# Three probability buffers instead of four in the first attention of a two-block transformer kernel

## Chip, core and metric

One Trainium2 chip, one of its cores. The metric is the device time of one launch in microseconds (us), the median of several runs. All arithmetic is float32, the large matrix products as three products of split operands. The engines that matter here are TensorE (PE), ScalarE (ACT), VectorE (DVE) and GpSimd (POOL). Each works through its own list of instructions in order and waits on semaphores that the others raise.

## What is computed

The reference is a chain of two transformer models of two layers each on 256 latent and 256 context tokens of width 1024. The change touches only the attention of the very first layer (`even_mixer`): eight heads of global grouped-query attention and eight heads of neighbourhood attention with a bias table, each over 512 keys for the latent tokens and over 256 keys for the context tokens. Cut to what matters:

```python
def gqa_scores(q, k):
    return jnp.einsum('bqkgd,btkd->bkgqt', q, k).astype(jnp.float32)

def gqa_out(p, v):
    return jnp.einsum('bkgqt,btkd->bqkgd', p.astype(v.dtype), v)

# global_gqa, heads 0..7 (latent queries see context and latent keys)
p = jax.nn.softmax(gqa_scores(q, k_all), axis=-1)
y = gqa_out(p, v_all)
# context queries see context keys alone
p = jax.nn.softmax(gqa_scores(qc, k_ctx), axis=-1)
y_ctx = gqa_out(p, v_ctx)
# neighbourhood_attention, heads 8..15: the same with a bias and a window on the latent keys
s_nb = jnp.einsum('brwhd,brwyxhd->bhrwyx', qblk, kn) + bias[None]
p = jax.nn.softmax(jnp.concatenate([s_nb, s_ctx], -1), axis=-1)
```

## The kernel before

The whole kernel is one long program for each engine: projections, attention, output rows, feed-forward layers, four times over. The change lies in the first attention stage, which in the profile runs from 134.6 to 226.5 us.

**Units.** The stage is cut into 24 units (`units_of("ev")`), three for each pair of heads: latent tokens 0 to 127 (t=0), latent tokens 128 to 255 (t=1), and all 256 context tokens (t=2, "context unit"). In units 0 to 11 the heads are global; from unit 12 on they are neighbourhood heads, whose t=0 and t=1 units are of the kind "rpb" (with the bias table). The words used below are: a *plain* unit is t=0 or t=1 of the first half, a *bias* unit is t=0 or t=1 of the second half.

**The steps of unit i.**

- scores(i), PE, L670: four matmuls of 256 columns (the trace counts eight records) into one of two pairs of PSUM banks. It waits for exp(i-2), which frees the banks.
- max(i), DVE: one `tensor_reduce` (L2272); for a bias unit a shorter `tensor_reduce` (L2264) and two fused add-and-reduce operations (L2269).
- exp(i), ACT, L1525: two activations of 512 columns, or four of 256 for a context unit, each with a row sum, from PSUM into a place for probabilities `A.P[slot]` in SBUF.
- normalise(i): DVE computes the reciprocals (L2284) and scales the first head (L2289: one operation of 512, or two of 256); POOL scales the second head (L2931).
- transposes(i), PE, L679: eight 128x128 transposes of the probabilities into PSUM banks 4 and 5.
- turned(i), ACT, L1515: two copies of the transposed probabilities to SBUF.
- values(i), PE, L692: the products with the values.
- After the third unit of a head pair: mixed_high on ACT (L1539) and mixed_low on DVE (L2296) split the result into two parts.

**What sets the order.** No scheduler: each engine's list is written by a loop over i, and the distance between the steps is `A.lag`, one less than the number of places in `A.P`. With four places, lag is 3. The loops in a pass i are, for PE: scores(i), `fill(i)`, transposes(i-lag), values(i-lag-1). For ACT: mixed_high(i-lag-2), turned(i-lag), exp(i), `fill(i)`. For DVE: normalise(i-lag+1), max(i), mixed_low(i-lag-2), `fill(i)`. For POOL: normalise(i-lag+1), `fill(i)`. These are the lines on DVE:

```python
            for i in range(A.n + A.lag + 2):
                if 0 <= i - A.lag + 1 < A.n:
                    normalise(i - A.lag + 1)
                ahead(i)
                if i < A.n:
                    softmax(i)
```

where `normalise(i)` begins with a wait for exp(i), and `softmax(i)` on DVE is max(i).

**What is filled in between.** PE computes a last projection (48 matmuls of 256 columns, L515 to L517) in pass 1 and again in pass 2, and twelve matmuls of the output rows (`first_rows_out`, the `drain`) in pass n+lag-1, before the last transposes. ACT rounds a half of an output weight block (L1467, `weights_half`) after exp(15), exp(17), exp(19) and exp(21), and DVE subtracts it (L1982) one pass later. POOL prepares the bias tables (L2968, `masks`): four in pass 5, two in pass 16, two in pass 19.

The four places are two in the arena (`P4a`), the scratch tile `tmp`, and a further piece of the arena at offset 18432. The second attention stage of the kernel ("od") has its own four places.

Of the kernel before, what the change touches and what calls it, by code (L numbers as in the profile page):

```python
# [144 lines left out]
def build_program(nc, T):  # L145
    with ExitStack() as ctx:
        _build(nc, T, ctx)


def _build(nc, T, ctx):  # L150
    def sb(name, shape, dt=F):
        return ctx.enter_context(nc.sbuf_tensor(name, shape, dt))
# [10 lines left out]
    tmp = sb("tmp", [128, 2, 512])  # L163
# [36 lines left out]
    def AR(off, *shape):  # L200
        n = int(np.prod(shape))
        v = arena[:, off:off + n]
        if len(shape) == 2:
            return v.rearrange("p (a b) -> p a b", a=shape[0])
        if len(shape) == 3:
            return v.rearrange("p (a b c) -> p a b c", a=shape[0], b=shape[1])
        if len(shape) == 4:
            return v.rearrange("p (a b c d) -> p a b c d", a=shape[0], b=shape[1], c=shape[2])
        return v
# [223 lines left out]
    class Att2:  # L433
# [38 lines left out]

    P4a = AR(0, 2, 2, 512)
    ATT = {
        "ev": Att("ev", "ev", [P4a[:, 0, :, :], P4a[:, 1, :, :], tmp[:, :, :], AR(18432, 2, 512)], [AR(2048, 2, 512), AR(6656, 2, 512)]),
        "od": Att("od", "od", [AR(6656, 2, 512), AR(7680, 2, 512), AR(4608, 2, 512), AR(10240, 2, 512)],
                  [AR(13312, 2, 512), AR(0, 2, 512)]),
    }
# [2816 lines left out]
```

## Time and profile before

| | us |
|---|---|
| median of 3 runs | 1568.55 |
| lowest and highest | 1568.24, 1570.21 |
| the profiled execution, its own time | 1568.17 |
| its span (first to last instruction) | 1566.7 |
| PE busy | 1545.5 |
| DVE busy | 1068.5 |
| ACT busy | 884.1 |
| POOL busy | 335.3 |

The profile is of one execution. Its span lies 1.5 us under that execution's own time, and that time lies 0.4 us under the median. A row of the timeline shows the start, the duration, the engine, the line of the kernel, the operation, the tiles (written <- read), how many instructions are merged in the row, and in brackets how long the engine was idle just before and what ended that. The ends of matmuls are modelled, so the pace of PE is read from start to start.

### The profile page before, as it was taken

What the parts mean: (1) busy time and instruction counts of PE and PEld (TensorE: products, weight loads), DVE (VectorE), ACT (ScalarE), POOL (GpSimd) and SP (SyncE); (2) the same over time, 40 slices, a digit from 0 to 9 for tenths busy, and PEclk for the clock granted to TensorE, in tenths of its full rate; (3) what the DMA queues carried; (4) which work ended last, traced back from release to release, by engine and by line L of the source; (5) the groups of instructions that cost most, each with busy time, mean ns of one, the idle gap of its engine ahead of it and who ended that gap; (6) DMA issues with size and microseconds to landing.
All of it is one profiled execution on the core that took longest, in us unless ns stands there. A gap on an engine that the chain in (4) does not pass through costs nothing.

```text
span 1566.7 us, 25547 instructions
## 1 busy us (share of the span) xinstructions
PE 1545.5 (99%) x9942; PEld 1321.7 (84%) x9942; DVE 1068.5 (68%) x1989; ACT 884.1 (56%) x1741; POOL 335.3 (21%) x338
## 2 busy tenths in 40 slices
PE   7999999999999999999999999999999999999998
PEld 4788778988887888887999988988888898888887
DVE  4743766666444435788887778777888668779875
ACT  2423874666652423568455555766666557667663
POOL 0201430465540000012011102142221014412210
PEclk9999999999999999999999999999999999999999
DMA  9767123345667233021456562434555534435552
GB/s 377 292 239 247 16 88 134 117 183 211 227 224 274 81 108 137 26 82 68 169 183 227 188 232 102 145 108 163 187 189 189 205 138 143 154 135 189 188 202 81
DMA packets 46951, 260.35 MB, mean 166 GB/s; under 512 B 11888, under 2 KB 13296, under 8 KB 18160
## 3 DMA queue, kind: packets, MB, share of 16 engines
q1 hardware_dynamic: 43808, 252.59, 44.3%
q0 software_dynamic: 1296, 4.72, 0.8%
q8 instruction: 79, 1.29, 0.4%
q10 hardware_dynamic: 1728, 1.43, 0.3%
q14 instruction: 40, 0.33, 0.1%
HBM read 257.64 MB, written 1.07 MB: 165 GB/s over the span
## 4 chain that ended last, share of the span: by engine, by line
PE 93%; DVE 3%; DMA 1%; ACT 1%; issue 1%; POOL 0%; DVEq 0%; ACTq 0%; POOLq 0%
PE ps L515 22%; PE ps L517 22%; PE ps L516 22%; PE ps L775 8%; PE ps L776 5%; PE ps L670 2%; PE ps L692 2%; PE ps L679 2%; PE ps L531 2%; PE ps L1187 1%; PE ps L777 1%; DMA raw<-in_ada 1%; PE ps L578 1%; PE ps L1198 1%; PE ps L1214 1%
## 5 line engine op out<-in xcount | busy, mean ns | idle before, releaser
L1976 DVE TENSOR_TENSOR wl<-raw,wh 128x1024 fp32r<-128x1024 f32 (+2 forms) x304 | 357.6, 1217 | 248.1 <-ACT wh L1460 246.0
L1460 ACT CAST wh<-raw 128x1024 fp32r<-128x1024 f32 (+2 forms) x314 | 309.4, 1035 | 332.1 <-PE ps L517 299.3
L515 PE MATMUL ps<-xx,wh 128*128 128x256 f32 (+1 forms) x1006 | 328.1, 326 | 0.0
L517 PE MATMUL ps<-xx,wl 128*128 128x256 f32 (+1 forms) x1006 | 325.5, 324 | 0.0
L516 PE MATMUL ps<-xx,wh 128*128 128x256 f32 (+1 forms) x1006 | 325.4, 323 | 0.0
L515 PE MATMUL ps<-wh,xx 128*128 128x512 f32 (+2 forms) x782 | 286.5, 366 | 1.8 <-issue 0.8
L517 PE MATMUL ps<-wh,xx 128*128 128x512 f32 (+2 forms) x782 | 281.5, 360 | 0.0
L516 PE MATMUL ps<-wl,xx 128*128 128x512 f32 (+2 forms) x782 | 281.4, 360 | 0.0
L2346 DVE SCALAR_TENSOR_TENSOR arena<-ps,pv,arena 128x254 f32<-128x254 f32 (+2 forms) x352 | 192.8, 548 | 28.7 <-ACT arena L1660 19.3
L515 PEld LDWEIGHTS ps<-xx,wh 128*128 128x128 f32 x1006 | 191.2, 190 | 20.0 <-issue 3.6
L517 PEld LDWEIGHTS ps<-xx,wl 128*128 128x128 f32 x1006 | 191.2, 190 | 15.2
L516 PEld LDWEIGHTS ps<-xx,wh 128*128 128x128 f32 x1006 | 191.3, 190 | 14.7
L2955 POOL TENSOR_TENSOR arena<-arena 128x256 f32<-128x256 f32 (+1 forms) x88 | 97.8, 1111 | 435.1 <-ACT arena L1637 435.0
L775 PE MATMUL ps<-xx,wh 128*128 128x512 f32 x504 | 180.8, 398 | 0.0
L515 PEld LDWEIGHTS ps<-wh,xx 128*128 128x128 f32 x782 | 147.6, 189 | 31.6 <-issue 10.0
L517 PEld LDWEIGHTS ps<-wh,xx 128*128 128x128 f32 x782 | 147.5, 189 | 21.5
L516 PEld LDWEIGHTS ps<-wl,xx 128*128 128x128 f32 x782 | 147.8, 189 | 20.4
L776 PE MATMUL ps<-xx,wl 128*128 128x256 f32 x576 | 150.0, 281 | 0.0
L2901 POOL TENSOR_TENSOR st<-st,cs 128x1 f32<-128x1 f32 (+2 forms) x44 | 35.6, 809 | 432.5 <-DVE st L2159 222.0
L1660 ACT ACTIVATE arena<-ps,pv 128x256 f32<-128x256 f32 (+1 forms) x176 | 98.8, 611 | 47.8 <-DVE ps L2336 42.7
L776 PEld LDWEIGHTS ps<-xx,wl 128*128 128x128 f32 x576 | 108.7, 189 | 6.8
L775 PEld LDWEIGHTS ps<-xx,wh 128*128 128x128 f32 x504 | 94.8, 188 | 19.7
(255 smaller groups left out, 2246.7 us busy)
## 6 DMA issues: line engine op xcount, KB each, us to landing
raw<-in_ada SPq DMA_DIRECT2D x46, 1024.0 KB, 5.2
raw<-in_up SPq DMA_DIRECT2D x44, 1024.0 KB, 4.8
raw<-in_fin SPq DMA_DIRECT2D x44, 1024.0 KB, 4.8
raw<-in_down SPq DMA_DIRECT2D x22, 1024.0 KB, 4.8
raw<-in_fout SPq DMA_DIRECT2D x22, 1024.0 KB, 4.8
raw<-in_win SPq DMA_DIRECT2D x12, 1024.0 KB, 5.0
raw<-in_ev_w_in SPq DMA_DIRECT2D x9, 1024.0 KB, 8.4
raw<-in_wout SPq DMA_DIRECT2D x8, 1024.0 KB, 4.8
```

Of the source, the lines that this page charges most:

```text
L515: e.matmul(out, A[0], B[0], start=first, stop=False)
L516: e.matmul(out, A[0], B[1], start=False, stop=False)
L517: return e.matmul(out, A[1], B[0], start=False, stop=last)
L531: m = e.matmul(ps[b][32 * g:32 * g + 32, 0:256], silp[:, k, 14 - 2 * i:46 - 2 * i], wv[:, k, :], start=(i == 0 and k < 4), stop=(last and ...
L775: e.matmul(both, hv[:, k, fs], xx[:, :, k, 0:256], start=k == 0, stop=False)
L776: m = e.matmul(both[:, 1, :], lv[:, k, fs], xh[:, k, 0:256], start=False, stop=False)
L1460: e.copy(hi_of(j)[:, a:b], raw_of(j)[:, a:b]).then_inc(*S.hi.up((j, half)))
L1660: e.activation(temp(up, f)[:, part, 0:n], ps[2 * (f % 3) + part][:, 0:n], ACT.Identity, bias=w[3], scale=w[1 if up[0] == "u" else 2]).then ...
L1976: e.tensor_tensor(lo_of(j)[:, a:b], raw_of(j)[:, a:b], hi_of(j)[:, a:b].bitcast(F), ALU.subtract).then_inc(*S.lo.up((j, half)))
L2346: e.scalar_tensor_tensor(acc[:, :, lo:hi], src[:, :, lo + shift:hi + shift], conv(row, f + NT * part), acc[:, :, lo:hi], ALU.mult, ALU.add ...
L2901: e.tensor_tensor(out, in_, minus_half[:, 0:n], ALU.pow).then_inc(*S.gps.up(key))
L2955: e.tensor_tensor((ACTF if ngrp == 2 else ACTF1)[:, f, 0:n], t[:, 1, 0:n], t[:, 0, 0:n], ALU.mult).then_inc(*S.prod.up((up, f)))
```

## The change

The tile `tmp` is taken out of the list of places for probabilities of the first attention.

```diff
     ATT = {
-        "ev": Att("ev", "ev", [P4a[:, 0, :, :], P4a[:, 1, :, :], tmp[:, :, :], AR(18432, 2, 512)], [AR(2048, 2, 512), AR(6656, 2, 512)]),
+        "ev": Att("ev", "ev", [P4a[:, 0, :, :], P4a[:, 1, :, :], AR(18432, 2, 512)], [AR(2048, 2, 512), AR(6656, 2, 512)]),
```

As `lag` is `len(P) - 1`, it becomes 2, and all loops of the stage are written with the shorter distance: PE has scores(i), transposes(i-2), values(i-3) in a pass; ACT has mixed_high(i-4), turned(i-2), exp(i); DVE has normalise(i-1), max(i), mixed_low(i-4); POOL has normalise(i-1). The number of operations, their shapes and their operands are the same but for the place they write. No transfer is moved on the DMA queue of SP.

DVE, in the first half of the stage. `128x4` marks a context unit (L2272 is its max, L2284 and L2289 its normalise), `128x2` another unit. Before:

```order
L2272 TENSOR_REDUCE st<-ps 128x4
L2284 RECIPROCAL st<-st 128x2
L2289 TENSOR_SCALAR arena<-arena,st 128x512
L2272 TENSOR_REDUCE st<-ps 128x2
L2284 RECIPROCAL st<-st 128x4
L2289 TENSOR_SCALAR arena<-arena,st 128x256 x2
L2272 TENSOR_REDUCE st<-ps 128x2
```

Now, at the same context unit (unit 5):

```order
L2272 TENSOR_REDUCE st<-ps 128x4
L2284 RECIPROCAL st<-st 128x4
L2289 TENSOR_SCALAR arena<-arena,st 128x256 x2
L2272 TENSOR_REDUCE st<-ps 128x2
L2296 TENSOR_TENSOR xx<-ps,xx 128x512
L2284 RECIPROCAL st<-st 128x2
```

The reciprocal of a unit stood behind the max of the unit after it; it now stands directly behind the unit's own max, and ahead of the next unit's max.

ACT, at the start of the stage: exp(0) and exp(1) are the `x4` row, L1450 copies the results of the projection filled in, L1515 is turned(0), and the row of 128x256 is exp(2).

```order
 L1525 ACTIVATE arena,st<-ps,st 128x512 x4
 L1450 COPY arena<-ps 128x256
-L1525 ACTIVATE tmp,st<-ps,st 128x256 x4
+L1515 COPY arena<-ps 128x512 x2
+L1525 ACTIVATE arena,st<-ps,st 128x256 x4
 L1450 COPY arena<-ps 128x256
 L1515 COPY arena<-ps 128x512 x2
```

turned(0) stood behind exp(2) and now stands ahead of it.

PE, at the end of the stage: L679 are transposes, L692 values, L515 the first matmul of the drain.

```order
 L692 MATMUL ps<-arena 64x128 x8
 L679 MATMUL ps<-cs,arena 128x128 x8
-L692 MATMUL ps<-arena 64x128 x8
-L679 MATMUL ps<-cs,tmp 128x128 x8
 L692 MATMUL ps<-arena 64x128 x8
 L515 MATMUL ps<-wh,xx 128x512
```

Behind the last scores there were two rounds of transposes and values ahead of the drain; there is now one.

## Rows read from the trace of the kernel before

**Rows 1.** The page, busy time and share of the span.

```profile
PE 1545.5 (99%) x9942; PEld 1321.7 (84%) x9942; DVE 1068.5 (68%) x1989; ACT 884.1 (56%) x1741; POOL 335.3 (21%) x338
```

**Rows 2.** Busy time by stretch: stretch, length, PE busy, PEclk, DMA share, GB/s.

```profile
0.00:10.00 10.00, 3.42 (x32) 1.00 0.85 314
...
134.60:226.50 91.90, 89.74 (x876) 1.00 0.34 100
```

**Rows 3.** The same with busy time of PE, PEld, DVE, ACT, POOL.

```profile
180.00:200.00 20.00, 20.00 (x213) 15.37 (x211) 16.33 (x45) 18.67 (x49) 8.16 (x10) 1.00 0.14 40
```

**Rows 4.** Timeline of PE, the scores of two units in a row.

```profile
184.37 1.13 PE L670 MATMUL ps<-arena 64*128 64x256 f32 x8
...
187.48 1.13 PE L670 MATMUL ps<-arena 64*128 64x256 f32 x8
```

**Rows 5.** Timeline of DVE: reciprocals, then the max of the next unit in the list.

```profile
195.05 0.16 DVE L2284 RECIPROCAL st<-st 128x2 f32<-128x2 f32 x1
...
195.65 1.22 DVE L2272 TENSOR_REDUCE st<-ps 128x4 f32<-128x1024 f32 x1
...
200.94 0.17 DVE L2284 RECIPROCAL st<-st 128x4 f32<-128x4 f32 x1
...
201.92 0.67 DVE L2264 TENSOR_REDUCE st<-ps 128x2 f32<-128x512 f32 x1
```

**Rows 6.** Timeline of ACT: first activation of an exp behind those maxima, and others.

```profile
153.09 0.70 ACT L1525 ACTIVATE arena<-ps,st 128x512 f32<-128x512 f32 x1
153.76 0.70 ACT L1525 ACTIVATE arena<-ps,st 128x512 f32<-128x512 f32 x1
...
196.90 0.47 ACT L1525 ACTIVATE arena<-ps,st 128x256 f32<-128x256 f32 x1 [0.36 <-DVE st L2272]
...
203.62 0.69 ACT L1525 ACTIVATE arena<-ps,st 128x512 f32<-128x512 f32 x1
...
216.16 0.47 ACT L1525 ACTIVATE arena<-ps,st 128x256 f32<-128x256 f32 x1 [0.33 <-DVE st L2272]
...
217.53 0.48 ACT L1525 ACTIVATE arena<-ps,st 128x256 f32<-128x256 f32 x1
```

**Rows 7.** Timeline of POOL and DVE: a scaling (reciprocals 214.32), the reciprocals of unit 23.

```profile
214.57 1.00 POOL L2931 TENSOR_SCALAR arena<-arena,st 128x512 f32<-128x512 f32 x1 [3.87 <-DVE st L2284]
...
218.13 0.18 DVE L2284 RECIPROCAL st<-st 128x4 f32<-128x4 f32 x1 [1.41 <-ACT arena L1525]
```

**Rows 8.** Timeline of PE and ACT, pass 3: scores, transposes, copies.

```profile
150.37 1.13 PE L670 MATMUL ps<-arena 64*128 64x256 f32 x8
151.43 1.09 PE L679 MATMUL ps<-cs,arena 128*128 128x128 f32 x8
...
152.12 1.07 ACT L1515 COPY arena<-ps 128x512 f32<-128x512 f32 x2 [4.13 <-PE ps L679]
```

**Rows 9.** Timeline of ACT, a weight half and the copies behind it.

```profile
198.72 1.05 ACT L1467 CAST wh<-raw 128x1024 fp32r<-128x1024 f32 x1
199.65 1.09 ACT L1515 COPY arena<-ps 128x512 f32<-128x512 f32 x2
```

**Rows 10.** Timeline of POOL and DVE, the four bias tables and a scaling beside them.

```profile
155.99 4.05 POOL L2968 TENSOR_TENSOR arena<-rows,arena 128x384 f32<-128x384 f32 x4
...
158.08 1.10 DVE L2289 TENSOR_SCALAR arena<-arena,st 128x512 f32<-128x512 f32 x1
```

**Rows 11.** Timeline of PE, the end of the stage.

```profile
218.72 1.12 PE L679 MATMUL ps<-cs,tmp 128*128 128x128 f32 x8 [1.09 <-DVE arena L2289]
...
220.79 0.50 PE L515 MATMUL ps<-wh,xx 128*128 128x512 f32 x1
...
226.51 0.50 PE L515 MATMUL ps<-wh,xx 128*128 128x512 f32 x1
```

**Rows 12.** Waits of PE and of SP's queue, whole span, longest groups: total, times, longest.

```profile
PE ps L531 <- DVE silp L2375: 6.6, 1, 6.6
...
SPq L58 <- DVE wl L1976: 908.6, 148, 39.9
```

## Prediction

> **What bounds the kernel now.** I read the page first: PE is busy for 1545.5 of 1566.7 us [rows 1], so a change counts only where it makes PE wait or saves it a wait. Over the stage that the change touches, PE is idle for 91.9 - 89.7 = 2.2 us [rows 2]; that is all that a better order could win there. In its timeline a pass of the stage (scores, transposes, values) takes 187.48 - 184.37 = 3.11 us and ends without a gap [rows 4]. So PE sets the pace, at 3.11 us a unit. The other engines are close behind in the later part: of 20 us ACT is busy for 18.67 and DVE for 16.33 [rows 3]. They keep up because four places let them work on different units at once. What the reader is to see next, in the timelines of DVE and ACT, is how long the steps of one unit take when each waits for the one before.
>
> **The change, part by part.** No operation is added or removed, so busy time moves nothing. What changes is the order, above all on DVE: normalise(i-1) now stands ahead of max(i), where normalise(i-2) stood. As normalise(i-1) starts with a wait for exp(i-1), and exp(i) waits for max(i), three steps form a closed loop, exp(i-1) -> reciprocals and scaling -> max(i) -> exp(i), of which nothing can overlap. Before, normalise(i-2) waited for an exp long done, and max(i) was free to run beside exp(i-1). What is queued behind the new wait on DVE is the max, then mixed_low and the weight half; ACT waits for the max, and PE for exp(i-2), which frees the score banks.
>
> *The length of the loop*, from start to start:
> - exp to reciprocals. Context unit: 216.16 to 218.13, 1.97 us [rows 6, 7]; its last activation starts at 217.53, lasts 0.48, and the reciprocals follow 0.12 behind its end. For two activations of 512 no reciprocal in the trace waits for its exp, so I build it: 0.67 to the second (153.09 to 153.76), 0.70 for it [rows 6], and the same 0.12: 1.49.
> - reciprocals to the next max: 0.60 (195.05 to 195.65), for a context unit with its two scalings 0.98 (200.94 to 201.92) [rows 5].
> - max to exp: 1.25 (195.65 to 196.90); for a bias unit 1.70 (201.92 to 203.62) [rows 5, 6].
>
> From exp to exp this makes 1.49 + 0.60 + 1.25 = 3.34 us between ordinary units and into a context unit; 1.97 + 0.98 + 1.25 = 4.20 from a context unit to a plain one; 1.49 + 0.60 + 1.70 = 3.79 into the second bias unit of a pair; 1.97 + 0.98 + 1.70 = 4.65 from a context unit to a bias one. All are over PE's 3.11, so from the first units on the loop sets the pace, and PE waits in every pass.
>
> *Is something on ACT longer than the loop?* Between two exps ACT makes the two copies of turned, 0.97 from their start to the exp (152.12 to 153.09) [rows 8, 6], and at four places a weight half, 0.93 (198.72 to 199.65) [rows 9]. Two activations hold ACT for about 2 x 0.67 = 1.34: 1.34 + 0.93 + 0.97 = 3.24, just under 3.34. So these stay hidden under DVE's part of the loop. If that cover fails they cost a tenth or two each, at four places. The copies wait for transposes(i-2); PE makes them after scores(i), which start when exp(i-2) ends, about 2 us behind it, and exp(i) comes over 5 us behind it. Hidden too, and so are values(i-3).
>
> *Start.* PE's projections in passes 1 and 2 (until 150.37) are unchanged. Now turned(0) stands ahead of exp(2) on ACT, and transposes(0) take PE's place at 150.37, where scores(3) stood [rows 8]. From the start of transposes to the copies it is 0.69 (151.43 to 152.12), to the exp 0.97 more: exp(2) starts at 150.37 + 1.66 = 152.03. The loop takes over from there.
>
> *The 21 steps from exp(2) to exp(23).* Into and out of context units and so on: 3 of 4.20, 10 of 3.34 (6 in the first half, 4 in the second), 4 of 3.79, 4 of 4.65: 12.60 + 33.40 + 15.16 + 18.60 = 79.76. exp(23) starts at 231.79; before it started at 216.16 [rows 6]. That is 15.6 later.
>
> *End.* The tail is shorter by one round, which gives some back. exp(22) starts 3.34 ahead of exp(23), at 228.45; its reciprocals are at 229.94; POOL's scaling ends 1.25 behind them (214.32 to 215.57) [rows 7], at 231.19. Then the second half of transposes(22) and values(21): half and whole of the 218.72 to 220.79 pair, 0.5 + 1.03, so the drain starts at 232.72. From the drain to the end of the stage PE's list is the same as before, 226.51 - 220.79 = 5.72 [rows 11]: 238.44, against 226.51. The stage ends **11.9 us later**. The 1.1 us wait at 218.72 [rows 11] is in these figures: it doesn't come back on its own.
>
> *The bias tables.* POOL prepares four in pass 5, one after another for 4.05 us; a scaling of DVE that met them took 1.10 us [rows 10], where it usually takes 0.49. Here nobody waited for it. With the change this block starts behind normalise(4), about 162.3, and normalise(5), two scalings in the loop, falls at about 165, still inside it. The row's surplus is 0.6; the bounds are 0 (the block has ended) and 1.3 (the time from 165.0 to the end of the block at 166.3). I take 0.6. The two blocks of two tables end before the next scaling; the weight half beside the first may meet it, for 0 to 0.6 us, and I take 0.
>
> The Trainium skill says on this ("SBUF — State Buffer", "Who interferes with whom") that VectorE's scaling between SBUF tiles can take a port pair which it shares with GpSimd, as an exclusive lock: the later one waits for the whole operation of the other. The row agrees. By that rule each of the two scalings could wait for a table of its own, which is the upper bound of 1.3 and would make the sum 13.2 instead of 12.5.
>
> *Behind the stage.* Does the rest give something back? Loads of weights wait for the engines that use the buffers, 908.6 us of SP's queue for one line alone [rows 12], not the other way round. The rest of the program shifts as a block. PE's idle time outside the stage is 21.2 - 2.2 = 19.0 us [rows 1, 2], its longest wait, 6.6 us [rows 12], ahead of the stage; even if all other 12.4 us of it were slack on something that runs on, they are waits for DVE and ACT by name, which shift too. I take 0.
>
> **Sum.** 11.9 + 0.6 = 12.5 us. Against the profiled execution's 1568.17 that is 1580.7; the median lies 0.4 above that execution: **1581.1 us**.
>
> **Rivals.**
>
> *PE keeps the pace (other side).* By shares of busy time no engine but PE is full, the transposes have a lead of two units left, and the loop would be no longer than PE's 3.11: then only the gap of 1.1 us at 218.72 would go [rows 11], 1567.5 us, no slower. This decides at one point: whether max(i) really stands behind the wait for exp(i-1), and whether 1.49 + 0.60 + 1.25 is under 3.11. The rows of DVE in the order say that it stands there, and each of the three figures but the 0.12 is read, so the sum can hardly lose 0.23. Even if it did, the steps behind context units and into bias units still cost 3 x 1.09 + 4 x 0.68 + 4 x 1.54 = 12.2, less 3.7 for the shorter end: 8.5 us. Chance 4%. The skill's rule that the engine with the highest occupancy is the one to look at ("Perfetto Trace Analysis", "Identifying Performance Opportunities") would lead here; the same section says that a gap which repeats can mean too few buffers, which is the forecast.
>
> *The loop is dearer than its parts.* Each hop costs 0.1 to 0.2 more when every step waits for a fresh semaphore, or ACT's weight halves and copies do end last. 21 x 0.15 = 3.2: 1584.3. Against it: the hops used are from rows with a wait in them (196.90, 218.13). Chance 14%.
>
> *The loop is cheaper.* A third of the steps lose 0.2 us, since a scaling or a max ends earlier than read, and the tables meet nothing: 1581.1 - 1.4 - 0.6 = 1579.1. Chance 12%.
>
> *PE's clock falls.* PE would be busy for some 84% of the stage, with gaps of up to 1.5 us in a pass. At 1.2 GHz a pass would take 6.2 us, over the loop: 20 passes x (6.2 - 3.8) = 48 us on top, 1629. Against it: in the first 10 us PE is busy for 3.42 and the granted clock is still 1.00, 2.4 GHz [rows 2], right through the wait of 6.6 us [rows 12]. Chance 2%.
>
> **How the numbers follow.** Forecast 68%, dearer 14%, cheaper 12%, other side 4%, clock 2%. The forecast's own bounds are 1580.5 (no table met) and 1582.4 (tables and weight half in full), and 1 us on each side for a twentieth of a us in the loop. With most of both neighbours the range is 1578.8 to 1585.0. A measurement of this kernel tells about 0.2%, 3.1 us, from no change; all cases but one lie over 10 us above: faster 0.01, same 0.04, slower 0.95.
>
> **What would show it.** In the new profile: reciprocals on DVE that wait for ACT L1525 in nearly every pass, and ACT L1525 for DVE's max; exps 3.3 and 4.2 us apart in the first half, 3.8, 3.3 and 4.7 in the second; PE idle ahead of L670 and L679 by some 15 us in the stage; exp(2) at 152.0, exp(23) at 231.8, the first matmul behind the stage at 239.0 (the tables included); after it, the same distances as before. I am wrong if PE passes of 3.11 us go on beyond pass 8, if ACT copies L1515 end last before the exps, or if the clock row shows less than 1.00.

## The result, and the profile of the changed kernel

The changed kernel takes 1581.47 us (median of 4 runs, 1581.32 to 1581.74), the kernel before 1569.38 us (4 runs, 1568.24 to 1570.59). The ratio is 1.0079, its 95% interval 1.0068 to 1.0091: about 12 us slower. The forecast was 1581.1 us, range 1578.8 to 1585.0. The profiled execution took 1581.32 us and its span is 1579.9 us, 13.2 us over the 1566.7 of before. Some 0.3 us of that lies ahead of the stage, whose first scores start at 134.90 instead of 134.60.

Busy time has not moved. The page of the changed kernel, the row that answers to [rows 1]:

```profile
PE 1545.1 (98%) x9942; PEld 1320.4 (84%) x9942; DVE 1069.5 (68%) x1989; ACT 883.7 (56%) x1741; POOL 335.7 (21%) x338
```

The stage now ends at 239.54 us. Busy time by stretch, with the columns of [rows 3]; the first row is before, the second the changed kernel:

```profile
134.60:226.50 91.90, 89.74 (x876) 71.80 (x876) 61.23 (x128) 70.51 (x191) 32.44 (x40) 1.00 0.34 100
...
134.60:239.00 104.40, 90.67 (x868) 71.23 (x870) 61.86 (x129) 71.09 (x191) 33.21 (x40) 1.00 0.29 89
```

PE was idle for 2.2 us of the stage and is now idle for 104.4 - 90.7 = 13.7 us. What it waits for is in the view of waits (total us, times, longest), changed kernel, of the stage:

```profile
POOL arena L2931 <- DVE st L2284: 111.8, 22, 49.4
DVE st L2284 <- ACT arena L1525: 32.0, 22, 2.9
ACT arena L1525 <- DVE st L2272: 14.7, 13, 2.6
...
PE ps L670 <- ACT arena L1525: 7.9, 14, 0.9
...
ACT arena L1525 <- DVE st L2269: 7.8, 8, 1.5
```

Three of these rows form a ring. DVE's reciprocals (L2284) wait for ACT's exp (L1525) 22 times; ACT's exp waits for DVE's max (L2272, L2269) 21 times; and max stands behind the reciprocals on DVE. In the same view of the kernel before, the first of these waits is

```profile
DVE st L2284 <- ACT arena L1525: 1.6, 2, 1.4
```

two waits instead of 22. PE waits outside the ring, most of all for the exp that frees its score banks: 7.9 of the 13.7 us. Ahead of its transposes (L679) it waits for another 3.7 us, for ACT's copies and for the scalings.

One turn of the ring in the timelines of DVE and ACT, changed kernel, plain units (start, duration, engine, line, operation; in brackets the idle time before):

```profile
172.87 0.17 DVE L2284 RECIPROCAL st<-st 128x2 f32<-128x2 f32 x1 [1.51 <-ACT arena L1525]
173.07 0.49 DVE L2289 TENSOR_SCALAR arena<-arena,st 128x512 f32<-128x512 f32 x1
173.47 1.22 DVE L2272 TENSOR_REDUCE st<-ps 128x4 f32<-128x1024 f32 x1
176.69 0.18 DVE L2284 RECIPROCAL st<-st 128x4 f32<-128x4 f32 x1 [2.00 <-ACT arena L1525]
...
171.39 0.69 ACT L1525 ACTIVATE arena<-ps,st 128x512 f32<-128x512 f32 x1 [0.93 <-DVE st L2272]
...
172.73 1.07 ACT L1515 COPY arena<-ps 128x512 f32<-128x512 f32 x2
174.73 0.48 ACT L1525 ACTIVATE arena<-ps,st 128x256 f32<-128x256 f32 x1 [0.93 <-DVE st L2272]
```

exp(7) starts at 171.39, the reciprocals 1.48 later, the max 0.60 later, exp(8) 1.26 later: 3.34 us. ACT had made its copies in between and then sat idle for 0.93 us; DVE sat idle for 1.51 us during the exp.

The end of the stage in the timeline of PE, changed kernel, which answers to [rows 11]:

```profile
231.63 1.22 PE L679 MATMUL ps<-cs,arena 128*128 128x128 f32 x8 [0.86 <-DVE arena L2289]
232.78 1.09 PE L692 MATMUL ps<-arena 128*64 128x128 f32 x16
233.80 0.50 PE L515 MATMUL ps<-wh,xx 128*128 128x512 f32 x1
...
239.54 0.50 PE L515 MATMUL ps<-wh,xx 128*128 128x512 f32 x1
```

From 239.54 to the end of the span it is 1340.4 us, from 226.51 in the kernel before 1340.2 us: the rest of the program is shifted as a block and gives nothing back (within 0.2 us).

### The profile page after: what moved, and what is told of

It is laid out like the page before. It is cut to its first block, busy times and chain, and to the rows that moved or that the text cites. A ratio compares the mean times of both kernels' runs of the same rounds, so it can differ in the third digit from the quotient of the medians.

```text
span 1579.9 us, 25547 instructions
## 1 busy us (share of the span) xinstructions
PE 1545.1 (98%) x9942; PEld 1320.4 (84%) x9942; DVE 1069.5 (68%) x1989; ACT 883.7 (56%) x1741; POOL 335.7 (21%) x338
## 4 chain that ended last, share of the span: by engine, by line
PE 90%; DVE 4%; ACT 2%; DMA 2%; issue 2%; POOL 0%; SPq 0%; DVEq 0%; ACTq 0%; POOLq 0%
PE ps L515 22%; PE ps L517 22%; PE ps L516 22%; PE ps L775 8%; PE ps L776 5%; ACT arena L1525 2%; PE ps L531 2%; PE ps L1187 1%; PE ps L692 1%; PE ps L670 1%; PE ps L679 1%; DMA raw<-in_ada 1%; PE ps L777 1%; PE ps L578 1%; DVE st L2272 1%
## 5 line engine op out<-in xcount | busy, mean ns | idle before, releaser
L515 PE MATMUL ps<-xx,wh 128*128 128x256 f32 (+1 forms) x1006 | 328.1, 326 | 0.0
L515 PE MATMUL ps<-wh,xx 128*128 128x512 f32 (+2 forms) x782 | 286.4, 366 | 2.8 <-DVE xx L2400 1.2
L515 PEld LDWEIGHTS ps<-xx,wh 128*128 128x128 f32 x1006 | 191.2, 190 | 20.2 <-issue 4.0
L515 PEld LDWEIGHTS ps<-wh,xx 128*128 128x128 f32 x782 | 147.5, 189 | 32.2 <-issue 8.3
```

The costliest lines, as they stand in the source:

```text
L515: e.matmul(out, A[0], B[0], start=first, stop=False)
```

## Experiments

All times are medians; the kernel before was run beside each group, at 1568.79, 1568.33 and 1567.91 us in the three of them, and each ratio is to that. The changed kernel was not run again, and the kernel before stood at 1569.38 us beside it, so a difference of one or two us between an experiment and the changed kernel's 1581.47 us can't be told from the times: there the traces decide. Line numbers below an inserted line are shifted in that run's rows. Theory A is the closed loop of the prediction; rival B is that three places, or PE's shorter lead, are too few whatever the order.

**The loop opened, with three places.** On DVE, for this stage alone:

```diff
-                if 0 <= i - A.lag + 1 < A.n:
+                if key == "od" and 0 <= i - A.lag + 1 < A.n:
                     normalise(i - A.lag + 1)
                 ahead(i)
                 if i < A.n:
                     softmax(i)
+                if key == "ev" and 0 <= i - A.lag + 1 < A.n:
+                    normalise(i - A.lag + 1)
```

> Three places as in the change, but DVE makes max(i) ahead of normalise(i-1) in a pass. Theory A (closed loop: the wait for exp(i-1) stands ahead of max(i)): the loop is open, exp(i) needs no step of unit i-1 but ACT itself, passes fall back to PE's 3.11 us and the time returns to 1569 to 1571 us (1.5 us stay for exp(2), which still waits for transposes(0)). Rival B (three places and a lead of two units are too few whatever the order): 1580 to 1582 us, passes of 3.3 us and more.

Measured: 1571.11 us, ratio 1.0015 (1.0006 to 1.0025), a tenth of a us over the expected 1569 to 1571. Ten of the twelve us are gone though nothing but two steps of DVE changed places. Its DVE timeline and a piece of PE's, passes of the first half:

```profile
173.56 1.23 DVE L2272 TENSOR_REDUCE st<-ps 128x2 f32<-128x1024 f32 x1 [1.29 <-PE ps L670]
174.70 0.17 DVE L2284 RECIPROCAL st<-st 128x4 f32<-128x4 f32 x1
...
176.67 1.23 DVE L2272 TENSOR_REDUCE st<-ps 128x2 f32<-128x1024 f32 x1 [0.32 <-PE ps L670]
...
172.38 1.13 PE L670 MATMUL ps<-arena 64*128 64x256 f32 x8
...
175.49 1.13 PE L670 MATMUL ps<-arena 64*128 64x256 f32 x8
```

DVE waits for PE again, not for ACT, and passes take 3.11 us. B is refuted as the main cause. What remains are 2.3 us. In the trace PE has waits that it didn't have before, 1.9 us in 4 times for POOL's scaling and 0.7 us for ACT's copy behind exp(2), and has lost the 1.1 us wait of [rows 11] but for 0.3: about 1.8 us of the 2.3.

**The loop closed, with four places.** DVE and POOL take `normalise(i - 1)` for this stage instead of `normalise(i - A.lag + 1)`; all else is the kernel before. The lines of DVE, POOL's being changed alike:

```diff
-                if 0 <= i - A.lag + 1 < A.n:
-                    normalise(i - A.lag + 1)
+                d = 1 if key == "ev" else A.lag - 1
+                if 0 <= i - d < A.n:
+                    normalise(i - d)
```

> Four places and all distances of the kernel before, but DVE and POOL make normalise(i-1) ahead of max(i) instead of normalise(i-2). Theory A: the same loop of 3.34, 4.20, 3.79 and 4.65 us from exp(3) on; exp(2) is not held back by transposes(0), so about 2.5 us less than the change: 1578 to 1579.5 us. Rival B (number of places and PE's lead decide): as before, 1568 to 1570 us.

Measured: 1582.15 us, ratio 1.0083 (1.0068 to 1.0098). The mechanism is the one expected, four places don't help; but my figure was 3 us too low. The timeline shows the missing term:

```profile
231.95 0.18 DVE L2284 RECIPROCAL st<-st 128x4 f32<-128x4 f32 x1 [2.00 <-ACT arena L1525]
...
231.79 1.08 ACT L1515 COPY arena<-ps 128x512 f32<-128x512 f32 x2
...
232.53 1.11 PE L679 MATMUL ps<-cs,tmp 128*128 128x128 f32 x8 [0.53 <-DVE arena L2289]
...
240.32 0.50 PE L515 MATMUL ps<-wh,xx 128*128 128x512 f32 x1
```

exp(23) starts 1.97 ahead of its reciprocals, at 229.98, and the stage ends at 240.32, 10.34 later, to 0.01 what the kernel before takes from there (216.16 to 226.51). The changed kernel takes 239.54 - 232.74 = 6.80. I had set 6.65 for the end here, that of a distance of two. With three, turned(21), which frees the banks of the transposes, stands behind exp(23) on ACT (231.79), and transposes(22) (232.53) wait for its first copy. The row of transposes(22) names DVE's L2289 instead, and so does [rows 11], but the scalings of unit 22 were done by 229.4; of the operations that they wait for by the code, only that copy ends just before. So the shorter distance gives back 3.5 us at the end, which the other order of DVE alone doesn't.

**Four places, distance two.** `self.lag = 2` and slots taken modulo four.

```diff
-            self.lag = len(P) - 1
+            self.lag = 2 if key == "ev" else len(P) - 1
...
-            return i % (self.lag + 1)
+            return i % len(self.P)
```

> Four places kept, but the distance (lag) is set to 2 as in the change. Theory A: only the order counts, not the places: as the change, 1581 to 1582 us. Rival B in its form that exp waits for a place to come free: with the fourth place that wait is gone, 1568 to 1572 us.

Measured: 1581.26 us, ratio 1.0077 (1.0062 to 1.0092), that of the change; in the trace exp(2) to exp(23) take 80.56 us, in the changed kernel 80.57. Taking the place away costs nothing by itself; the distance that the code derives from it does. This run lengthens the distance between writes to a place but keeps the wait of exp(i) for transposes(i-3), so it tells of the order and not of that wait; the run with the loop opened, which has three places and the wait, shows that it costs nothing that matters.

**The loop made longer.**

```diff
+                for _ in range(2 if key == "ev" else 0):
+                    e.reciprocal(rc, sm).then_inc(*S.vec.up())
+                    q.wait_ge(*S.vec.last())
                 e.reciprocal(rc, sm).then_inc(*S.vec.up((key, "rc", i)))
```

In the changed kernel:

> The change, with the reciprocals of each unit made three times instead of once (two more operations of about 0.20 us from start to start, in the supposed loop). Theory A: every one of 21 steps is 0.4 us longer, 8.4 us in all: 1590 us. Rival (the loop has slack, PE or ACT sets the pace): 1581 to 1583 us.

Measured: 1590.25 us, 8.8 over the changed kernel (1589.43 to 1590.93). Two exps in its ACT timeline, then PE at the end of the stage:

```profile
172.88 0.69 ACT L1525 ACTIVATE arena<-ps,st 128x512 f32<-128x512 f32 x1 [1.32 <-DVE st L2272]
...
176.62 0.47 ACT L1525 ACTIVATE arena<-ps,st 128x256 f32<-128x256 f32 x1 [1.32 <-DVE st L2272]
...
239.65 1.21 PE L679 MATMUL ps<-cs,arena 128*128 128x128 f32 x8 [1.66 <-DVE arena L2292]
240.79 1.75 PE L692 MATMUL ps<-arena 128*64 128x128 f32 x16
...
249.12 0.50 PE L515 MATMUL ps<-wh,xx 128*128 128x512 f32 x1
```

3.74 us instead of 3.34, and ACT's idle time grows by the same 0.4. So do 20 of the 21 steps; the one from exp(5) to exp(6) stays at 5.03, as there the tables hold DVE's scalings, which end 0.65 us behind the last table in either run. exp(2) to exp(23) take 88.74 us instead of 80.57: all that is put in the ring goes to the end, 8.2 us. The time agrees with the expected 1590 us partly by luck, for something else is in it: from exp(23) at 240.77 to the end of the stage at 249.12 it is 8.35 us instead of 6.80, because TensorE's clock fell there (the last section); without that this execution would have been 1.5 us shorter.

The same edit in the kernel before:

> The kernel before (four places), with the reciprocals made three times, 0.4 us more of DVE for each of 24 units. Theory A: no closed loop there, DVE's 2.3 us a pass become 2.7 and stay under PE's 3.11; only where the weight halves load DVE late in the stage may it show: 1568.5 to 1570.5 us. If it costs 8 us or more, the kernel before had no slack on DVE and the loop is no property of the change.

Measured: 1570.84 us, ratio 1.0016 (1.0007 to 1.0025): 2.5 us for the same 9.6 us of work on DVE, and 0.3 over what I had allowed. In the view of waits of that run, of the stage, and the longest of these waits in PE's timeline:

```profile
PE ps L679 <- ACT arena L1515: 2.6, 4, 1.4
...
220.69 1.12 PE L679 MATMUL ps<-cs,tmp 128*128 128x128 f32 x8 [1.43 <-ACT arena L1515]
```

The longest stands at the place of the 1.1 us wait of [rows 11], so the new ones come to about 1.5 us. So before the change DVE had slack of 0.4 us in most passes; after it, in none.

**exp(2) ahead of turned(0).** On ACT, in pass 2 of this stage alone, `turned(0)` is moved from ahead of exp(2) to behind the fill:

```diff
+                late = key == "ev" and i == A.lag
-                if 0 <= i - A.lag < A.n:
+                if 0 <= i - A.lag < A.n and not late:
                     turned(i - A.lag)
...
                 fill(i)
+                if late:
+                    turned(i - A.lag)
```

> The change, but in pass 2 ACT makes exp(2) ahead of turned(0). Theory A with its start term: exp(2) is done long before PE's projections end, exp(3) starts at 154.0 instead of 156.4 and all that follows 2.4 us earlier: 1579 us. Rival (the start is made up for later, PE was behind anyway until pass 8): 1581 to 1582 us.

Measured: 1579.38 us (1579.29 to 1579.82, 5 runs), ratio 1.0071 (1.0058 to 1.0083). ACT's timeline (L2275 is max here):

```profile
146.15 0.47 ACT L1525 ACTIVATE arena<-ps,st 128x256 f32<-128x256 f32 x1 [2.24 <-DVE st L2275]
...
154.31 0.70 ACT L1525 ACTIVATE arena<-ps,st 128x512 f32<-128x512 f32 x1
```

exp(3) starts at 154.31 instead of 156.36, 2.05 earlier, exp(23) 2.03 earlier, and the span is 2.1 shorter (1577.8 against 1579.9). Once the ring sets the pace, what is late at its start is never made up for.

**The bias tables in pass 2**, `masks({2: range(4), 16: (4, 5), 19: (6, 7)}...)` for `{5: range(4), ...}` on POOL.

> The change, but POOL prepares the first four bias tables in pass 2, where DVE and POOL are idle for the projections, instead of pass 5. If the two scalings of unit 5 (1.69 us instead of 0.85) were held by the tables, they fall back to 0.85, the step exp(5) to exp(6) from 5.03 to 4.20, and the stage ends 0.8 us earlier: 1580.6 us. If not, nothing moves.

Measured: 1586.51 us, 1582.89 to 1588.95, ratio 1.0114: slower by 5, not faster by 0.8. The profile is of the fastest execution, 1582.89. Its timelines of POOL, PE and DVE:

```profile
151.81 1.00 POOL L2968 TENSOR_TENSOR arena<-rows,arena 128x384 f32<-128x384 f32 x1 [6.64 <-DMA arena<-in_rpb]
155.35 1.00 POOL L2968 TENSOR_TENSOR arena<-rows,arena 128x384 f32<-128x384 f32 x1 [2.54 <-DMA arena<-in_rpb]
156.70 1.94 POOL L2968 TENSOR_TENSOR arena<-rows,arena 128x384 f32<-128x384 f32 x2 [0.36 <-DMA arena<-in_rpb]
...
159.78 1.12 PE L679 MATMUL ps<-cs,arena 128*128 128x128 f32 x4 [2.77 <-POOL arena L2931]
...
167.63 0.85 DVE L2289 TENSOR_SCALAR arena<-arena,st 128x256 f32<-128x256 f32 x2
```

I had looked only at when POOL is idle, not at when the tables have landed. They come in between 151 and 157 us; POOL waits for them with the scalings of units 2 and 3 queued behind, and PE waits 2.77 us for that of unit 2. The other half of the expectation did come true: with no table in pass 5 the two scalings of unit 5 take 0.85 us (167.63), and exp(5) to exp(6) is 4.21 us instead of 5.03. That is hidden in the time by the larger loss ahead of it. That the executions differ by 6 us because the transfers land at different times is likely, but not shown: only one was profiled.

**The tables spread**, one in each of passes 4 to 7.

```diff
-masks({5: range(4), 16: (4, 5), 19: (6, 7)}.get(i, ()))
+masks({4: (0,), 5: (1,), 6: (2,), 7: (3,), 16: (4, 5), 19: (6, 7)}.get(i, ()))
```

> The change, with the first four bias tables made one a pass in passes 4 to 7, behind POOL's scaling. Theory A with its term for the tables: a table ends about 2.3 us behind the reciprocals of its pass, before the next scaling at 3.3, so the two scalings of unit 5 take 0.85 us instead of 1.69, the step from exp(5) to exp(6) is 4.20 instead of 5.03 us, and the time falls by 0.8 us to about 1580.6. Rival (the 0.84 us come from something other than the tables): the step stays 5.03.

Measured: 1580.48 us (1580.40 to 1580.63), ratio 1.0078 (1.0063 to 1.0094), 1.0 under the changed kernel, which the times alone can't show. First the changed kernel's DVE row of the two scalings of unit 5 and the POOL row beside it, then the same scalings of this run:

```profile
165.21 1.69 DVE L2289 TENSOR_SCALAR arena<-arena,st 128x256 f32<-128x256 f32 x2
...
162.39 3.86 POOL L2968 TENSOR_TENSOR arena<-rows,arena 128x384 f32<-128x384 f32 x4
```

```profile
165.26 0.84 DVE L2289 TENSOR_SCALAR arena<-arena,st 128x256 f32<-128x256 f32 x2
```

The tables do hold DVE's scalings: 0.85 us, in the ring, once. exp(5) to exp(6) is 4.18 us here (163.08 to 167.26) and 5.03 in the changed kernel. Not all of it is won: exp(4) to exp(5) is 3.60 us here instead of 3.33, for a reason that no row names. The stage ends at 238.75 instead of 239.54, 0.8 us earlier, of which 0.2 lie ahead of the stage.

**All together, with three places:** max ahead of normalise, exp(2) ahead of turned(0), and all eight tables in passes of their own (4 to 7, 16, 17, 19, 20).

> Three places, max(i) ahead of normalise(i-1), exp(2) ahead of turned(0), and all eight tables spread over passes of their own. Theory A: the loop is open, the start gives back the 0.7 us that PE waited for the copy behind exp(2), and the spread tables give back the 1.0 us and more that PE waited for POOL: about 1568.5 to 1569.5 us, within 0.1% of the kernel before with one place less, so `tmp` is free. Rival (three places leave PE too little lead even so): 1571 us, as with max ahead alone.

Measured: 1569.18 us, ratio 1.0008 (1.0000 to 1.0017): 1.3 us over the kernel before, at the edge of what can be told from it. In the profiled execution, the fastest of 11 with 1568.28 us, the stage ends at 226.45, before at 226.51. So three places are enough for PE's pace. It doesn't beat four: PE had 2.2 us of idle time to win in the stage, and there was nothing else in it.

## Why the prediction was right

- **The bound.** PE at 3.11 us a pass with the others close behind: the opened loop falls back to exactly that.
- **The loop and its lengths.** Read from rows of a kernel in which the loop didn't exist, they held to 0.02 in all steps but two. The 20 steps from exp(3) at 156.36 to exp(23) at 232.74 are 3.33 to 3.35 where 3.34 was set (and 3.86 once, for 3.79, in the late part), 4.19 for 4.20, 4.63 to 4.65 for 4.65, and 5.03 at the tables. The 3.86 is DVE's own: its weight half and mixed_low ran until 215.34 and held the reciprocals by 0.07, where the prediction had sized the weight halves on ACT alone. From exp(2) at 152.17 it is 80.57 us in all; 79.76 was set without the tables, 80.60 with their measured 0.84. The part that had no row, 1.49 from an exp of two activations to the reciprocals, is 1.48.
- **What ACT hides.** Copies and weight halves stay under DVE's part: ACT is idle for 0.93 us ahead of an exp in an ordinary step, and 0.44 or less beside a weight half. Only exp(20), at 220.98, follows its copies without a gap: 3.24 against 3.34 had left a tenth, and there it was used up.
- **The start.** exp(2) at 152.17, set at 152.03; PE's projections ended 0.2 later in this execution. The run with exp(2) ahead of turned(0) shows that this term is real. I hadn't seen that PE would wait 0.73 us for ACT's copy behind exp(2); PE had time for it. That PE would wait in every pass from the first units on was not so: passes 4 and 5 took 3.12 and 3.11 us without a wait, while PE used up its lead; the exps kept the ring's pace from exp(2) on.
- **The end.** 6.80 us from exp(23), set at 6.65. The give-back was right; its reason, turned(21) behind exp(23) in the order before, I learned only when I left it out of an expectation.
- **The tables.** 0.85 where I took 0.6, between the bounds of 0 and 1.3. The Trainium skill's rule of an exclusive lock ("SBUF — State Buffer", "Who interferes with whom") agrees with the row of 1.69 us and with the 0.84 once the tables are spread; two scalings that each met a whole table would have cost more.
- **Behind the stage.** Nothing was given back, as set.
- **The rivals.** That PE keeps the pace was tested by the order of DVE and is false with the change's order and true with the other. That a gap which repeats means too few buffers, which the prediction equated with its forecast, is not so here: four buffers in the closed order cost as much as three, and three in the open order cost 2.3 us. For the same reason it is not the four places as such that let the engines keep up before. That the clock falls did not happen in this kernel's stage, but see below: the argument against it was weak. PE's busy share, set at some 84%, comes to 86% by the prediction's own figures (89.7 of 104.4 us) and was 87%.

The errors of the start, the steps and the end, 0.1 to 0.2 us each and all of one sign, add to half a us in the stage (239.54 against 239.0). That the time is nearer still, 0.4 us, is luck: the profiled execution was set at 1580.7 and took 1581.32, and the 0.4 that was added to get from it to a median was only 0.15 here.

## What to carry to other kernels

When the distance between steps of a software pipeline is derived from a number of buffers, a buffer less is a change of order: write down each engine's list for two passes and look for a ring, a step that waits for another engine and stands ahead of the step that this engine waits for. The length of such a ring can be added up from the rows of a trace in which it doesn't exist, to a few hundredths of a us, and it counts from the first pass in which it is longer than the bound engine's pass. Before giving a buffer back or asking for one more, try swapping the two steps in the ring.

## What the runs showed of the hardware

TensorE's clock fell in three of the experiments, and with shorter gaps than I had thought harmless. Four places with the loop closed, PE by stretch of 2 us (length, PE busy, granted clock, DMA share, GB/s):

```profile
198.00:200.00 2.00, 1.41 (x20) 1.00 0.04 8
200.00:202.00 2.00, 1.14 (x8) 1.00 0.00 0
202.00:204.00 2.00, 1.61 (x8) 0.58 0.02 4
204.00:206.00 2.00, 2.00 (x20) 0.56 0.54 153
206.00:208.00 2.00, 2.00 (x18) 1.00 0.12 40
```

and the waits and durations in its PE timeline:

```profile
200.39 1.14 PE L670 MATMUL ps<-arena 64*128 64x256 f32 x8 [0.98 <-ACT arena L1525]
202.38 1.94 PE L679 MATMUL ps<-cs,tmp 128*128 128x128 f32 x8 [0.86 <-DVE st L2269]
204.25 1.80 PE L692 MATMUL ps<-arena 128*64 128x128 f32 x16
205.99 1.13 PE L670 MATMUL ps<-arena 64*128 64x256 f32 x8
```

After two waits of 0.98 and 0.86 us in one pass, with PE busy for 2.55 of 4 us, the granted clock went from full (2.4 GHz) to little over half over the two stretches (1.2 GHz for most of them), and eight transposes took 1.94 instead of 1.09 us; at 226 us it happened again. Here the ring covers the loss: exp(17), at 206.38, waited for DVE, whose max stood directly behind its scaling. In the run with the tables in pass 2 it fell behind the wait of 2.77 us. In the run with the longer loop it fell behind the 1.66 us wait at 239.65, where PE had been busy for 0.35 of the 2 us from 238: granted clock 0.77 from 240 to 242 us and 0.50 from 242 to 244, values(21) in 1.75 instead of 1.09 us, and the first twelve matmuls of the drain in 3.79 instead of 2.88 us. There nothing covers it: it is at the end of the stage. In the changed kernel the granted clock of the stage is 1.00; its worst pass there has waits of 0.65 and 0.86 us, 1.5 us against the 1.84 above. What exactly decides between the two is left open. My rival for the clock had rested on a row at the start of the program, where PE is idle and the clock still full; that row was no witness for the middle of a stage.

POOL's tables and DVE's weight half, which both read two tiles of SBUF, also hold each other. First the changed kernel, then four places with the loop closed, two tables beside a weight half:

```profile
205.61 1.22 DVE L1982 TENSOR_TENSOR wl<-raw,wh 128x1024 fp32r<-128x1024 f32 x1
...
204.69 3.00 POOL L2968 TENSOR_TENSOR arena<-rows,arena 128x384 f32<-128x384 f32 x2
```

```profile
203.10 1.52 DVE L1982 TENSOR_TENSOR wl<-raw,wh 128x1024 fp32r<-128x1024 f32 x1
...
201.58 1.96 POOL L2969 TENSOR_TENSOR arena<-rows,arena 128x384 f32<-128x384 f32 x2
```

In the changed kernel two tables took 3.00 us instead of the 1.96 they take alone, while DVE's operation, which started ahead of the second table, kept its 1.22. This is the meeting for which the prediction allowed 0 to 0.6 us and took 0: it fell on POOL's side, off the ring, and cost nothing. That was luck. In the other run the tables were under way first and kept their 1.96 us, DVE's operation took 1.52, and the step from exp(16) to exp(17) is 3.70 us instead of 3.35: there it is in the ring and costs 0.35, a second, smaller part of what my figure for that run was too low by.
